# Expert weight slots fetched as two half transfers, each with its own semaphore and its own release

## The chip, the cores and the metric

One program on one core of a Trainium2 chip. The metric is the device time of one execution in microseconds; the times below are of three runs. The profile is of one further execution on the same kind of core, with the TensorE clock that was granted to it.

## What is computed

One decoder layer on 1024 tokens of width 1024, in float32. A first part mixes tokens (an RG-LRU branch, sliding-window attention, cross-attention to 256 memory tokens, one output projection). The second part, in which the change lies, is a mixture of 32 experts, four per token:

```python
def expert_block(args):                      # one block of up to 128 tokens of expert e
    xblk, e = args
    h = xblk @ w1[e] + b1[e]                 # w1[e]: 1024 x 2048
    return clamped_swiglu(h) @ w2[e] + b2[e] # w2[e]: 1024 x 1024

yb = lax.map(expert_block, (xb, block_expert)).reshape(P, D)
out = jnp.zeros((N, D), jnp.float32).at[tok_buf].add(yb.astype(jnp.float32) * gate_buf[:, None])
```

## The kernel before, in words

Each engine has an instruction stream written out by hand; semaphores tie them. From about 583 us a loop over passes runs on every engine (`Fori(0, total)`). A pass takes one expert and either one block of 128 tokens (`body((0,))`) or two (`body((0, 1))`), which is decided at run time by a table in SBUF. Here there are 32 passes, 19 with one block and 13 with two.

**Weights.** An expert is 12 MB: `NSLOT` = 12 slots of 1 MB, eight of w1 (four chunks of 128 rows by 512 columns) and four of w2 (two chunks of 128 rows by 1024 columns). A slot has two halves, `h = 2 * s` and `2 * s + 1`, and `part(h)` names the SBUF words of one. The raw words land in `ring`, which has room for `RAW` = 6 slots. SyncE (SP) issues a slot's transfer in `load_slot` (L379 to L385) and does nothing else in the loop: for each of the 12 slots it waits at L416 until the slot's place is free (`raw_done[s % RAW]`, counted up by one for each half), then issues (L385) with `slot_in[s % RAW]` as its semaphore. It works up to six slots ahead and goes on into the next pass's expert.

**Splitting.** A product in full precision is made of three float32r products. So each half is copied by ScalarE (ACT) into a rounded high part (`split_hi`, L760 to L769, into a ring of `SPLIT` = 8 buffers `w_hi`), after a wait for the slot's landing (L763) and for TensorE to have used the buffer (`w_used`, L765). VectorE (DVE) subtracts to get the low part (`split_lo`, L1688 to L1696, helper line L1643, into `w_lo`), and that operation counts `raw_done` up. Six halves at the start are split at L738 and L524. In passes with one block, slots 8 and 10 (`WHOLE`) aren't split: TensorE multiplies them as plain float32 straight out of `ring` (L1246), and releases the whole slot at its end by adding 2 to `raw_done` (L1248).

**TensorE (PE)** does per pass `up` or `up_turned` for w1, then `down` for w2. `wait_words` (L1158 to L1163) is its wait for a half: for `raw_done` or, where the slot is whole, for `slot_in`. The three products are L1138, L1139 and L1140.

**Tokens.** GpSimd (POOL) gathers the rows of the next pass, `xg`, by indirect DMA (L516) and adds the result rows to `out` by an indirect DMA that accumulates (the scatter, L549), in this order in a pass: `idx_cur` (L538), gather, scatter, wait for the scatter. TensorE transposes the gathered rows (L1132) after a wait at L1282 in the middle of the pass. The chain from the end of one pass is: ScalarE's `combine` writes `y` (L802), scatter, `idx_cur`, VectorE's `idx_next` (L1639), gather, transposes. All these transfers and the weights share the core's 16 DMA engines.

At the end VectorE waits for the transfers still in flight, one wait and one memset per semaphore (L1792 to L1794).

Of the kernel before, what the change touches and what calls it, by code (L numbers as in the profile page):

```python
# [40 lines left out]
HALF = 512  # L41
# [8 lines left out]
NSLOT = 12  # L50
NPART = 2 * NSLOT
RAW = 6
# [18 lines left out]
def hymba_layer(nc, x, mem, g_mix, w_in, conv_w, conv_b, lru_wa, lru_ba, lru_wx, lru_bx, lru_lambda,  # L71
# [3 lines left out]
    with ExitStack() as ctx:  # L75
# [3 lines left out]
        def sem(name):  # L79
            return ctx.enter_context(nc.semaphore(name))  # L80
# [25 lines left out]
        credit = sb("credit", [P, 16])  # L106
# [135 lines left out]
        ex_in, ex_done, mask_ready, pos_done, gates_ready, gt_done, gt_out, init_mm, init_ready = map(  # L242
            sem, "ex_in ex_done mask_ready pos_done gates_ready gt_done gt_out init_mm init_ready".split())
        ptab_ready, ttab_ps, ttab_ready = sem("ptab_ready"), sem("ttab_ps"), sem("ttab_ready")
        slot_in = [sem(f"slot_in{i}") for i in range(RAW)]
        hi_ready = sem("hi_ready")
        raw_done = [sem(f"raw_done{i}") for i in range(RAW)]
        w_used, y_half = sem("w_used"), sem("y_half")
# [74 lines left out]
        def slot(s):  # L323
            return ring[:, (s % RAW) * SLOT:(s % RAW + 1) * SLOT].rearrange("p (k c) -> p k c", k=4)
# [19 lines left out]
        @block.sync  # L344
        def _(sp):
            load_vectors(sp, 0)
            sp.dma_start(mem_sb, mem[0].rearrange("(t p) d -> p t d", p=P)).then_inc(mem_in, 16)
            xv = x[0].rearrange("(t p) d -> p t d", p=P)
            sp.dma_start(w_mem, w_mem_kv[0].rearrange("(k p) c -> p k c", p=P)).then_inc(w_mem_in, 16)
            sp.dma_start(xh[:, 0:4, :], xv[:, 0:4, :]).then_inc(x_in[0], 16)  # L350
            wv = w_in[0].rearrange("(k p) c -> p k c", p=P)
            def load_wA(i):
                sp.dma_start(wA[i], wv[:, :, i * DL:(i + 1) * DL]).then_inc(wA_in[i], 16)

            load_wA(0)
            sp.dma_start(xh[:, 4:8, :], xv[:, 4:8, :]).then_inc(x_in[1], 16)
            for i, (a, b, c) in enumerate(((384, 512, 1152), (0, 384, 768), (512, 768, 1408))):
                sp.dma_start(wB[:, :, a:b], wv[:, :, c:c + b - a]).then_inc(wB_in[i], 16)
            load_wA(1)

            sp.dma_start(wV, wv[:, :, 1280:1408]).then_inc(wout_in, 16)

            sp.wait_ge(normed, 2)
            sp.wait_ge(kz_zero, 5)
            for g in range(2):
                for half in range(2):
                    sp.dma_start(kz[g][half][half * DH:(half + 1) * DH, :],
                                 uT[g * DH:(g + 1) * DH, K, :]).then_inc(kz_in, 16)
            sp.wait_ge(spread, len(norm_units))
            sp.wait_ge(scanned, LT)  # L370
            for i in range(2):
                sp.dma_start(xh[:, 4 * i:4 * i + 4, :], xv[:, 4 * i:4 * i + 4, :]).then_inc(x_again[i], 16)
            sp.wait_ge(in_done, len(units))
            sp.dma_start(w_out_sb, w_out[0].rearrange("(k p) c -> p k c", p=P)).then_inc(wout_in, 16)

            w1v = w1[0].rearrange("e (k p) c -> e p k c", p=P)
            w2v = w2[0].rearrange("e (k p) c -> e p k c", p=P)

            def load_slot(e, s):  # L379
                if s < 8:  # L380
                    src = w1v[bass.ds(e, 1), :, 4 * (s % 2):4 * (s % 2) + 4, HALF * (s // 2):HALF * (s // 2) + HALF]
                else:
                    src = w2v[bass.ds(e, 1), :, 2 * (s - 8):2 * (s - 8) + 2, :]
                dst = slot(s) if s < 8 else slot(s).rearrange("p (k b) c -> p k (b c)", k=2)
                sp.dma_start(dst, src.rearrange("o p k c -> (o p) k c")).then_inc(slot_in[s % RAW], 16)  # L385


            sp.wait_ge(ylru, LT)
            sp.dma_start(gbc, g_ffn.to_broadcast([P, D])).then_inc(gbc_in, 16)

            sp.wait_ge(lru_ss, 1)
            sp.wait_ge(yt_out, ytc[-1])
            sp.wait_ge(o_ss, len(items))
            for s in range(4):
                load_slot(0, s)
            sp.wait_ge(op_done, 6 * NT)
            sp.wait_ge(padded, 2)
            sp.dma_start(b2_sb[0:E, :], b2[0]).then_inc(b2_in, 16)
            sp.wait_ge(b1_zero, 1)
            for half in range(2):  # L400
                sp.dma_start(b1_raw[half * E:(half + 1) * E, :], b1[0]).then_inc(b1_in, 16)
            sp.wait_ge(ttab_ready, 1)
            for s in range(4, RAW):
                load_slot(0, s)
            for i in range(NT):
                sp.wait_ge(init_ready, 2 * i + 2)
                sp.dma_start(out[0, i * P:(i + 1) * P, :], xh[:, i, :]).then_inc(init_out, 16)
            sp.wait_ge(init_out, 16 * NT)
            total = sp.value_load(ttab[0:1, TALL:TALL + 1], min_val=1, max_val=NPASS)
            with sp.Fori(0, total) as p:  # L410
                e_now = sp.value_load(ttab[0:1, bass.ds(p + TE, 1)], min_val=0, max_val=E - 1)
                e_next = sp.value_load(ttab[0:1, bass.ds(p + (TE + 1), 1)], min_val=0, max_val=E - 1)

                for s in range(RAW, RAW + NSLOT):

                    sp.wait_ge(raw_done[s % RAW], p * (NPART // RAW) + 2 * (s // RAW))  # L416
                    load_slot(e_now if s < NSLOT else e_next, s % NSLOT)

        @block.gpsimd
        def _(po):  # L420
# [143 lines left out]
        def _(act_e):  # L564
# [169 lines left out]
            act_e.wait_ge(w_used, SPLIT)  # L734
            act_e.preload_act_table(ACT.Gelu_apprx_sigmoid)
            for s in range(LEAD):
                act_e.wait_ge(slot_in[s // 2], 16)
                act_e.activation(halves_of(w_hi[s][:, :, :]), pairs_apart(part(s)), ACT.Copy).then_inc(hi_ready, 1)  # L738
            act_e.wait_ge(ttab_ready, 1)
            take_xhi(1, 0, 4)  # L740
# [9 lines left out]
            with act_e.Fori(0, total) as p:  # L750
# [6 lines left out]
                def body(groups):  # L757
                    whole = whole_of(groups)

                    def split_hi(s):  # L760
                        if s in whole:
                            return
                        act_e.wait_ge(slot_in[s % RAW], p32 + 16 * (s // RAW + 1))  # L763
                        for h in (2 * s, 2 * s + 1):
                            act_e.wait_ge(w_used, p24 + (h + 1 - (SPLIT if s - SPLIT // 2 in whole else 0)))  # L765
                            hi, raw = w_hi[h % SPLIT][:, :, :], part(h)
                            if s % NSLOT < 8:
                                hi, raw = halves_of(hi), pairs_apart(raw)
                            act_e.activation(hi, raw, ACT.Copy).then_inc(hi_ready, counted(h, whole))  # L769
# [62 lines left out]
        def _(pe):  # L832
# [313 lines left out]
            with pe.Fori(0, total) as p:  # L1146
# [8 lines left out]
                def body(groups):  # L1155
                    whole = whole_of(groups)

                    def wait_words(h):  # L1158
                        s = h // 2
                        if s in whole:  # L1160
                            pe.wait_ge(slot_in[s % RAW], p32 + 16 * (s // RAW + 1))
                        else:
                            pe.wait_ge(raw_done[s % RAW], uses + (2 * (s // RAW) + h % 2 + 1))  # L1163

# [143 lines left out]
        def _(dve):  # L1308
# [480 lines left out]
                with dve.Else():  # L1789
                    body((0,))  # L1790

            for i in range(RAW):  # L1792
                dve.wait_ge(slot_in[i], total * 32 + 16)
                dve.memset(credit[:, 8 + i:9 + i], 0.0)  # L1794


# [22 lines left out]
```

## Time and profile before

| | |
|---|---|
| three runs, us | 2244.38, 2245.2, 2251.28; median 2245.2 |
| profiled execution: its own time | 2243.14 us |
| profiled execution: span from first to last instruction | 2241.4 us |
| mean granted TensorE clock | 0.981 of full speed |
| TensorE busy | 2152.1 us (96% of the span) |
| VectorE, ScalarE busy | 1415.9 us, 1133.2 us |
| weight transfers issued by SyncE | 390 of 1024.0 KB, median 7.1 us from issue to landing |
| all DMA traffic | 477.64 MB, mean 213 GB/s |

The profile is of one execution. Busy times of engines overlap, so their sum says nothing; what matters is where TensorE, the busiest, stands idle and what ended the idle time. A matmul's end is modelled, so the spacing of starts tells its pace better than its duration. "Landing" is the time from a transfer's issue to its semaphore.

### The profile page before, as it was taken

The page shows a single profiled execution, that of the slowest core. Times are in us where ns is not written, and L with a number is a line of the kernel's source. Part 1 is how long each engine was busy: PE and PEld are TensorE (multiplying, and loading weights), DVE is VectorE, ACT ScalarE, POOL GpSimd, SP SyncE. Part 2 cuts the span into 40 slices and gives each one's busy share as a digit, 9 for nine tenths or more (in the row PEclk, how much of TensorE's full clock was granted, in tenths as well). Part 3 has the DMA queues.
Part 4 walks back from the last instruction along what each step waited for, and adds up shares of the span by engine and source line. Part 5 has one row for each costly group of instructions (what it writes and reads, how often), then busy time and mean ns, then how long its engine had stood idle before and what let it go on. Part 6 is the DMA issues. An engine that isn't in the chain of part 4 may idle for free.

```text
span 2241.4 us, 34981 instructions
## 1 busy us (share of the span) xinstructions
PE 2152.1 (96%) x11402; PEld 1675.3 (75%) x11403; DVE 1415.9 (63%) x2192; ACT 1133.2 (51%) x1570; POOL 217.6 (10%) x208
## 2 busy tenths in 40 slices
PE   6999988996999999999999999999999999999997
PEld 4443776443579977887797979887779888898895
DVE  3242574334676578768767676768886667667665
ACT  3241353112365567556646565556765555555555
POOL 2000200001300111010101010101110100101001
PEclk9999998996899999999999999999999999999998
DMA  7000402002696669968959595868998568659656
GB/s 260 1 0 19 160 1 76 28 29 71 241 349 236 215 218 359 335 207 319 370 210 312 190 322 181 316 195 310 353 351 299 192 204 295 200 181 319 190 191 218
DMA packets 203190, 477.64 MB, mean 213 GB/s; under 512 B 14743, under 2 KB 20951, under 8 KB 203088
## 3 DMA queue, kind: packets, MB, share of 16 engines
q1 hardware_dynamic: 185662, 437.95, 54.0%
q0 software_dynamic: 17424, 39.17, 7.3%
q8 instruction: 24, 0.39, 0.1%
q14 instruction: 14, 0.11, 0.0%
q10 hardware_dynamic: 66, 0.02, 0.0%
HBM read 468.73 MB, written 32.11 MB: 223 GB/s over the span
## 4 chain that ended last, share of the span: by engine, by line
PE 84%; DMA 7%; issue 3%; DVE 3%; ACT 2%; POOLq 1%; POOL 0%; ACTq 0%; DVEq 0%; SPq 0%
PE ps L1138 18%; PE ps L1140 18%; PE ps L1139 18%; PE ps L902 7%; PE ps L1246 6%; PE ps L1056 5%; DMA out<-y,idx_cur 3%; DMA xg<-token_rows,idx_next 3%; PE ps L1132 2%; PE ps L1007 1%; PE ps L975 1%; PE ps L1176 1%; PE ps L1196 1%; PE ps L1118 1%; PE ps L1075 1%
## 5 line engine op out<-in xcount | busy, mean ns | idle before, releaser
L769 ACT ACTIVATE w_hi<-ring 128x1024 fp32r<-128x1024 f32 x692 | 745.2, 1123 | 456.7 <-PE ps L1140 386.0
L1643 DVE TENSOR_TENSOR w_lo<-ring,w_hi 128x1024 fp32r<-128x1024 f32 x692 | 816.5, 1221 | 205.8 <-ACT w_hi L769 205.8
L1138 PE MATMUL ps<-xT,w_hi 128*128 128x256 f32 x1248 | 354.2, 284 | 0.0
L1140 PE MATMUL ps<-xT,w_lo 128*128 128x256 f32 x1248 | 353.1, 283 | 0.0
L1139 PE MATMUL ps<-xT,w_hi 128*128 128x256 f32 x1248 | 353.1, 283 | 0.0
L1138 PE MATMUL ps<-w_hi,xT 128*128 128x512 f32 x816 | 320.8, 393 | 6.3 <-issue 4.6
L1139 PE MATMUL ps<-w_lo,xT 128*128 128x512 f32 x816 | 319.8, 392 | 0.0
L1140 PE MATMUL ps<-w_hi,xT 128*128 128x512 f32 x816 | 319.3, 391 | 0.0
L1139 PEld LDWEIGHTS ps<-xT,w_hi 128*128 128x128 f32 x1248 | 239.5, 192 | 0.5
L1138 PEld LDWEIGHTS ps<-xT,w_hi 128*128 128x128 f32 x1248 | 239.4, 192 | 0.5
L1140 PEld LDWEIGHTS ps<-xT,w_lo 128*128 128x128 f32 x1248 | 239.4, 192 | 0.0
L1138 PE MATMUL ps<-w_hi,actT 128*128 128x512 f32 x568 | 231.9, 408 | 0.0
L1140 PE MATMUL ps<-w_hi,actT 128*128 128x512 f32 x568 | 221.9, 391 | 0.0
L1139 PE MATMUL ps<-w_lo,actT 128*128 128x512 f32 x568 | 221.4, 390 | 0.0
L549 POOL DMA_INDIRECT out<-y,idx_cur x45 | 82.8, 1840 | 1101.2 <-ACT y L802 1045.0
L1138 PEld LDWEIGHTS ps<-w_hi,xT 128*128 128x128 f32 x816 | 154.0, 189 | 41.7 <-DVE xT L1643 5.6
L1140 PEld LDWEIGHTS ps<-w_hi,xT 128*128 128x128 f32 x816 | 153.8, 188 | 32.9
L1139 PEld LDWEIGHTS ps<-w_lo,xT 128*128 128x128 f32 x816 | 153.7, 188 | 32.7
L1246 PE MATMUL ps<-ring,actT_f 128*128 128x512 f32 x304 | 136.7, 592 | 0.0
L1139 PEld LDWEIGHTS ps<-w_lo,actT 128*128 128x128 f32 x568 | 106.8, 188 | 25.6 <-issue 4.5
L1138 PEld LDWEIGHTS ps<-w_hi,actT 128*128 128x128 f32 x568 | 106.7, 188 | 25.2 <-issue 4.5
L1711 DVE TENSOR_SCALAR hm<-ps,km 128x256 f32<-128x256 f32 x156 | 64.7, 478 | 94.5 <-PE ps L1140 94.5
(274 smaller groups left out, 2417.4 us busy)
## 6 DMA issues: line engine op xcount, KB each, us to landing
ring<-in_w SPq DMA_DIRECT2D x390, 1024.0 KB, 7.1
xh<-in_x SPq DMA_DIRECT2D x4, 2048.0 KB, 15.5
work<-in_w_out SPq DMA_DIRECT2D x1, 4096.0 KB, 12.7
token_rows<-uT POOLq DMA_DIRECT2D x8, 512.0 KB, 2.9
out<-xh SPq DMA_DIRECT2D x8, 512.0 KB, 2.7
work<-in_w_in SPq DMA_DIRECT2D x2, 1536.0 KB, 18.4
uT<-in_w_mem_kv SPq DMA_DIRECT2D x1, 2048.0 KB, 13.8
ring<-in_w_in SPq DMA_DIRECT2D x1, 1536.0 KB, 18.4
```

The costliest lines, as they stand in the source:

```text
L549: po.indirect_dma_start(out=out[0], out_offset=by_index(idx_cur, g), in_=y[:, g, :], in_offset=None, bounds_check=last_row, oob_is_err=Fal ...
L769: act_e.activation(hi, raw, ACT.Copy).then_inc(hi_ready, counted(h, whole))
L902: m = pe.matmul(ps[:, unit_bank(i), :], w[:, k, :], xnT[:, k, h * HALF:(h + 1) * HALF], start=k == 0, stop=k == KD - 1)
L975: m = pe.matmul(ps[:, u % 4, n * 256 + lo:n * 256 + 256], qs, keys, start=True, stop=True)
L1056: m = pe.matmul(ps[:, 2 * g + half, :], uT[:, c, i * P:(i + 1) * P], w_out_sb[:, kk + n, half * HALF:(half + 1) * HALF], start=n == 0, sto ...
L1132: m = pe.transpose(ps[:, bank + k // 4, k % 4 * P:(k % 4 + 1) * P], xg[:, g, k * P:(k + 1) * P], ident[:, :])
L1138: pe.matmul(acc, hi, whi, start=first, stop=False, skip_group_check=shared)
L1139: pe.matmul(acc, hi, wlo, start=False, stop=False, skip_group_check=shared)
L1140: return pe.matmul(acc, lo, whi, start=False, stop=last, skip_group_check=shared)
L1246: m = pe.matmul(acc, actT_f[:, j + k, :], slot(s)[:, 2 * k + b, :], start=first, stop=last)
L1643: return dve.tensor_tensor(lo, x, hi.bitcast(F32), ALU.subtract)
L1711: m = dve.tensor_scalar(hm[:, g, j % 2, cols], ps[:, 2 * (j % 2) + g, cols], b1_cols[:, 4 * j + 2 * g + o, bass.ds(e, 1)], LIMIT + o, ALU. ...
```

## The change

A slot is now two transfers of 512 KB, one for each half. There are 12 semaphores `slot_in` in place of six, one for each half of the ring. SyncE waits for a half's release ahead of that half's transfer, ScalarE waits for a half's landing ahead of that half's copy, TensorE likewise for the unsplit slots. The bytes, their places in SBUF and all arithmetic are the same. The diff, with nothing but repeated context left out:

```diff
-        slot_in = [sem(f"slot_in{i}") for i in range(RAW)]
+        slot_in = [sem(f"slot_in{i}") for i in range(2 * RAW)]
...
-            def load_slot(e, s):
+            def load_half(e, h):
+                s = h // 2
                 if s < 8:
-                    src = w1v[bass.ds(e, 1), :, 4 * (s % 2):4 * (s % 2) + 4, HALF * (s // 2):HALF * (s // 2) + HALF]
+                    k0 = 4 * (s % 2) + 2 * (h % 2)
+                    src = w1v[bass.ds(e, 1), :, k0:k0 + 2, HALF * (s // 2):HALF * (s // 2) + HALF]
                 else:
-                    src = w2v[bass.ds(e, 1), :, 2 * (s - 8):2 * (s - 8) + 2, :]
-                dst = slot(s) if s < 8 else slot(s).rearrange("p (k b) c -> p k (b c)", k=2)
-                sp.dma_start(dst, src.rearrange("o p k c -> (o p) k c")).then_inc(slot_in[s % RAW], 16)
+                    src = w2v[bass.ds(e, 1), :, h - 16:h - 15, :]
+                return src.rearrange("o p k c -> (o p) k c")
+
+            def load_slot(e, s, freed=None):
+                for h in (2 * s, 2 * s + 1):
+                    if freed is not None:
+                        sp.wait_ge(raw_done[s % RAW], freed + h % 2)
+                    dst = part(h) if s < 8 else part(h).rearrange("p (k b) c -> p k (b c)", k=1)
+                    sp.dma_start(dst, load_half(e, h)).then_inc(slot_in[h % (2 * RAW)], 16)
...
-                    sp.wait_ge(raw_done[s % RAW], p * (NPART // RAW) + 2 * (s // RAW))
-                    load_slot(e_now if s < NSLOT else e_next, s % NSLOT)
+                    load_slot(e_now if s < NSLOT else e_next, s % NSLOT, p * (NPART // RAW) + (2 * (s // RAW) - 1))
...
             for s in range(LEAD):
-                act_e.wait_ge(slot_in[s // 2], 16)
+                act_e.wait_ge(slot_in[s], 16)
...
-                        act_e.wait_ge(slot_in[s % RAW], p32 + 16 * (s // RAW + 1))
                         for h in (2 * s, 2 * s + 1):
+                            act_e.wait_ge(slot_in[h % (2 * RAW)], p32 + 16 * (s // RAW + 1))
...
-                            pe.wait_ge(slot_in[s % RAW], p32 + 16 * (s // RAW + 1))
+                            pe.wait_ge(slot_in[h % (2 * RAW)], p32 + 16 * (s // RAW + 1))
...
-            for i in range(RAW):
+            for i in range(2 * RAW):
                 dve.wait_ge(slot_in[i], total * 32 + 16)
-                dve.memset(credit[:, 8 + i:9 + i], 0.0)
+                if i % 2:
+                    dve.memset(credit[:, 8 + i // 2:9 + i // 2], 0.0)
```

How the streams stand, first SyncE in its loop, at slots 6, 7 and 8 (`raw_done0` to `raw_done2` are the places of the ring, 128x4x512 is partitions x chunks x columns; L385 is the line of the issue). Before:

```order
L385 ISA [waits raw_done0]
L385 DMA ring<-in_w 128x4x512
L385 ISA [waits raw_done1]
L385 DMA ring<-in_w 128x4x512
L385 ISA [waits raw_done2]
L385 DMA ring<-in_w 128x2x1024
```

The same three slots with the change, where the issue has line L393:

```order
L393 ISA [waits raw_done0]
L393 DMA ring<-in_w 128x2x512
L391 REGISTER_ALU
L393 ISA [waits raw_done0]
L393 DMA ring<-in_w 128x2x512
L393 ISA [waits raw_done1]
L393 DMA ring<-in_w 128x2x512
L393 ISA [waits raw_done1]
L393 DMA ring<-in_w 128x2x512
L393 ISA [waits raw_done2]
L393 DMA ring<-in_w 128x1024
L393 ISA [waits raw_done2]
```

Each transfer has become two with a wait ahead of each, and the rows that one moves are as long as before (512 or 1024 words). Then ScalarE in its loop, at the splits of slots 4 and 5 in a pass with two blocks. Before, one wait for a slot and a register operation without a wait ahead of its second half:

```order
L769 ACTIVATE w_hi<-ring 128x1024 [waits w_used]
L765 REGISTER_ALU [waits slot_in5]
L769 ACTIVATE w_hi<-ring 128x1024 [waits w_used]
L765 REGISTER_ALU
L769 ACTIVATE w_hi<-ring 128x1024 [waits w_used]
```

With the change (L772 and L776 are the same two statements):

```order
L776 ACTIVATE w_hi<-ring 128x1024 [waits w_used]
L772 REGISTER_ALU [waits slot_in10]
L776 ACTIVATE w_hi<-ring 128x1024 [waits w_used]
L772 REGISTER_ALU [waits slot_in11]
L776 ACTIVATE w_hi<-ring 128x1024 [waits w_used]
```

The second register operation now holds the wait for the second half; no instruction has been added or moved in the loop. TensorE's, VectorE's and GpSimd's compute instructions stand in the same order as before.

## Rows read from the trace of the kernel before

**Rows 1.** The page, part 1: busy time, share of the span, instructions.
```profile
PE 2152.1 (96%) x11402; PEld 1675.3 (75%) x11403; DVE 1415.9 (63%) x2192; ACT 1133.2 (51%) x1570; POOL 217.6 (10%) x208
```

**Rows 2.** Expert loop: length, busy (x) of PE, PEld, DVE, ACT, POOL; clock, DMA share, GB/s.
```profile
600.00:2227.00 1627.00, 1621.06 (x9312) 1360.15 (x9310) 1152.81 (x1688) 949.91 (x1176) 154.05 (x139) 1.00 0.76 264
```

**Rows 3.** TensorE's waits from 600 us on: us in total, times, longest.
```profile
PE ps L1132 <- DMA xg<-token_rows,idx_next: 4.1, 7, 1.3
PE ps L1138 <- DVE hm L1716: 1.2, 1, 1.2
```

**Rows 4.** The chain that ended last: start, us, what (first, steady run, last).
```profile
612.66 3.44 PE ps L1246 x8
...
1599.46 3.44 PE ps L1246 x8
...
1636.88 3.43 PE ps L1246 x8
...
1665.09 8.82 DMA xg<-token_rows,idx_next
1675.04 3.44 PE ps L1246 x8
...
2214.28 3.44 PE ps L1246 x8
```

**Rows 5.** ScalarE's waits for weights over the whole span.
```profile
ACT w_hi L769 <- DMA ring<-in_w: 57.3, 32, 4.6
```

**Rows 6.** Steady single-block passes, columns as in rows 2.
```profile
1551.00:1588.50 37.50, 37.50 (x174) 28.21 (x173) 30.74 (x44) 26.14 (x32) 3.85 (x4) 1.00 0.97 357
...
1626.00:1663.50 37.50, 37.50 (x174) 28.17 (x173) 30.84 (x44) 26.19 (x32) 3.93 (x4) 1.00 0.94 347
```

**Rows 7.** DMA view from 1575 to 1595 us; GB/s in 40 slices of 0.5 us.
```profile
GB/s 414 418 410 397 401 393 385 393 393 389 389 369 381 320 312 340 357 360 369 410 397 414 438 397 451 401 401 410 410 410 434 401 434 401 393 401 410 406 398 406
DMA packets 3100, 7.91 MB, mean 395 GB/s; under 512 B 240, under 2 KB 240, under 8 KB 3100
...
q1 hardware_dynamic: 2871, 7.49, 96.4%
...
ring<-in_w SPq DMA_DIRECT2D x8, 1024.0 KB, 12.2
xg<-token_rows,idx_next POOLq DMA_INDIRECT x2, 7.6
```

**Rows 8.** SyncE's waits from 600 us on.
```profile
SPq L385 <- DVE w_lo L1643: 1078.3, 248, 9.6
SPq L385 <- PE ps L1246: 283.7, 38, 12.4
```

**Rows 9.** Tile ring, then line L385: ns min/median/max, first and last start; landing in us.
```profile
L1643 DVE TENSOR_TENSOR w_lo<-ring,w_hi x692: 1205/1220/1286, 589.8 to 2226.8; 128x1024 fp32r<-128x1024 f32 x173
...
L385 SPq DMA_DIRECT2D ring<-in_w x390: 368/373/829, 376.7 to 2225.1; - x195
...
DMA to landing us min/median/max: 4.7/7.1/15.1
```

**Rows 10.** SyncE in order of time, 1612.4 to 1614.2 us.
```profile
1612.51 1.78 SPq L385 DMA_DIRECT2D ring<-in_w  x3
```

**Rows 11.** Landing of the gather (tile xg), then of the scatter (tile out), from 600 us.
```profile
DMA to landing us min/median/max: 3.1/5.9/8.9
...
DMA to landing us min/median/max: 6.0/7.9/9.6
```

**Rows 12.** TensorE's weight loads ahead of the transposes, from the waits.
```profile
PEld ps L1132 <- DMA xg<-token_rows,idx_next: 8.3, 10, 1.8
```

**Rows 13.** The end: VectorE and GpSimd in order of time.
```profile
2232.39 0.06 DVE L1794 MEMSET credit<- 128x1 f32 x1 [2.61 <-DMA ring<-in_w]
...
2228.67 1.62 POOL L549 DMA_INDIRECT out<-y,idx_cur  x1 [23.08 <-ACT y L802]
```

**Rows 14.** The page, part 6: a 512 KB transfer, KB, median us to landing.
```profile
out<-xh SPq DMA_DIRECT2D x8, 512.0 KB, 2.7
```

## The prediction

> **What bounds the kernel now.** I read the page's totals first, then busy time by stretch, then the waits, and at the end single passes.
>
> The page [rows 1] gives TensorE 2152.1 of 2241.4 us. By stretch [rows 2], the expert loop from 600 to 2227 us holds 1621.06 busy of 1627.00, at a granted clock of 1.00. So TensorE stands idle there for 1627.00 - 1621.06 = 5.9 us, and its waits [rows 3] name nearly all of it: 4.1 us in seven waits for the gathered token rows xg and 1.2 us in one for hm. No wait for a weight is in that list. A busy figure can hide a slow cadence, so I also looked at the chain of waits in a run of passes with one block each [rows 4]: the first eight fp32 matmuls of L1246 of a pass start at 1599.46 and 1636.88, a period of 37.4 us. The next ones start at 1675.04, 38.2 us later; this pass was held up, and by the gather that stands before it in the chain, which landed at 1665.09 + 8.82 = 1673.91.
>
> Who does wait for weights? ScalarE, 57.3 us in 32 waits, the longest 4.6 us [rows 5]. It may be 8 halves ahead of TensorE (the rings w_hi and w_lo), and none of these waits comes out on TensorE. The DMA engines are closer to a limit than the page's mean says: 0.76 busy over the loop [rows 2], but 0.97 to 0.94 in the three steady passes of the run [rows 6], of which the first and the last stand there. In a stretch of 20 us the rate stays between 312 and 451 GB/s with some seven slots passing through [rows 7]. SyncE mostly waits for a free slot: 1078.3 + 283.7 = 1362 of the loop's 1641 us [rows 8].
>
> So there are two quantities near a limit: TensorE, and in runs of single-block passes the DMA engines, on which also hangs the chain y, scatter, gather, transposes.
>
> **The change part by part.**
>
> *Twice the transfers.* 390 become 780, 24 in a pass in place of 12. The order of instructions shows the same bytes in the same row lengths (128x2x512 for 128x4x512, 128x1024 for 128x2x1024), so the engines' data packets are as many. On SyncE an issue takes 0.373 us [rows 9], and three in a row with their register work 1.78 us [rows 10], 0.6 us each. 12 more in each of 32 passes make 384 x 0.6 = 230 us, against 1362 us of waiting: SyncE's queue hides it. A half moves for about 512 KB / 395 GB/s = 1.3 us (the rate from [rows 7]), twice its issue, so a burst stays limited by the engines, too. Were this cover gone, 12 x 0.6 = 7 us a pass would show.
>
> *What a boundary between transfers costs on the engines.* No row shows it alone. From below: zero, for in [rows 7] whole half-microsecond slices stand at 401 to 451 GB/s and no dip recurs every 2.6 us. From above: charge all that the 20 us lack against the fast slices of some 415 GB/s, (415 - 395) / 415 = 5%, or 1.0 us, to 7.5 boundaries: 0.13 us each. Twelve more in a pass are then 0 to 1.6 us of engine time. The steady passes have 3 to 6% of 37.5 us free, 1.1 to 2.2 us. I take zero, as the slices without a dip are the nearest row; even the upper end just fills what is free.
>
> The Trainium skill ("DMA: Bandwidth & Descriptors", section Rules for kernel authors) speaks against the change: it asks for at least 1 MiB per DMA, and its Anatomy section puts a fixed 2.0 us on each. Its formula would give 4.4 us for a slot and 2 x 3.2 = 6.4 us for two halves, an estimate from that page, if they went one by one; the trace does not agree that this sets the pace, since twelve slots pass in 37.5 us with other traffic beside them.
>
> *The release by half.* VectorE's two w_lo operations on a slot take 1.22 us each [rows 9], and SyncE no longer waits for the second: the first half of a slot is asked for about 1.2 us sooner. Not so for slots 8 and 10 of single-block passes, which the matmuls of L1246 release as a whole (38 of SyncE's waits, [rows 8]). The data starts sooner only where engines are idle at that time.
>
> *The wait by half.* ScalarE can split a first half when that has landed, some 1.3 us before its slot would have. That can take up to 32 x 1.3 = 42 us out of its 57.3 us. By the order of instructions it costs nothing: the register operation ahead of the second half now carries the wait that it lacked, and no row is added. What does it give TensorE? Nothing directly, since TensorE never waits for a weight. Indirectly, VectorE's low parts come sooner behind ScalarE's high ones, again ahead of need. The one wait for hm is the only place where this could reach TensorE.
>
> *What could shift on the path.* Scatter and gather. The gather's landing ranges from 3.1 to 8.9 us, median 5.9; the scatter's from 6.0 to 9.6, median 7.9 [rows 11]. Weight traffic that starts 1.2 us sooner also ends sooner where a refill runs out during the gather. At best all 4.1 + 1.2 = 5.3 us go. At worst every critical gather is like the slow ones: in the steady run it landed in 7.6 us [rows 7], in the pass that was held up in 8.8 [rows 4]; 1.2 us more at each of the 10 single-block passes in which the transposes' weight loads already wait for it [rows 12], 12 us. I take -0.5 us: the traffic at those places is saturated in both kernels, and bytes per pass are the same.
>
> *Prologue and end.* The first slot is issued at 376.7 us [rows 9], long ahead of the loop; nothing waits for the first halves. At the end the last two refills are issued by 2225.1, VectorE takes the second at 2232.39 [rows 13], and the kernel closes with a scatter issued at 2228.67, which at the shortest landing of a scatter, 6.0 us [rows 11], is still under way at 2235. Two issues more are 2 x 0.6 = 1.2 us, in front of something that has over 2 us to spare. Zero; if the cover were gone, 1.2 us.
>
> **Sum.** 0 (issue) + 0 (boundaries) + 0 (ScalarE's waits) - 0.5 (gather) + 0 (end) = -0.5 us. The profiled execution took 2243.14 us by its own time, so it would take 2242.6. The median of the three runs is 2.1 us above that execution; against it the forecast is 2244.7 us. 0.3% of the time is 6.7 us, as much as the three runs spread (2244.38 to 2251.28), and about what a measurement tells from no change. So: no change.
>
> **Rivals.**
>
> 1. *The gather pays (slower).* Halves asked for sooner keep weight packets queued at the very time the scatter and the gather want the 16 engines. Place: the wait for xg at L1282 in single-block passes. Price: up to 1.2 us in 10 passes, 12 us, 2257 us. It decides from the point where scatter and gather together land over 0.7 us later, for 10 x 0.7 is 7 us. For it: in the steady run the transposes come right as the gather lands. Against it: weight traffic is at 96% there already [rows 7], and cannot crowd more.
>
> 2. *The boundary costs (slower).* If a boundary took 0.25 us, twelve would be 3.0 us against about 1.6 free: 1.4 us for each of the 9 single-block passes that follow another such pass, 13 us, 2257 us (19 such passes start between 612.66 and 2214.28, [rows 4], in ten runs, the longest of five). It needs twice my upper bound. Driven to its end, with each transfer waiting for the one before, it would be 24 x 2.7 us (the landing of a 512 KB transfer, [rows 14]) = 65 us for a single-block pass in place of 37.5, some 19 x 27 = 520 us, 2765 us. But by that reading the kernel before would need 12 x 4.7 (the shortest landing of a slot, [rows 9]) = 56 us for a pass, and it takes 37.5; I give this end 0.005. It is what the Trainium skill's fixed cost per DMA, named above, would mean here.
>
> 3. *Relief (faster).* The sooner loads end before the gather does and clear its waits wholly, 5.3 us, with a shorter last scatter perhaps 7 us: 2238 us. For it: the waits are there. Against it: the share of the engines stays 0.94 and more.
>
> 4. *The change does not do what it says.* A half is free early only where VectorE frees it; if VectorE's pair comes back to back and the queue of weights is deep anyway (12.2 us to land in the steady run, [rows 7]), the sooner request buys nothing. The time is then 2245.2, within the forecast.
>
> **Chances.** Forecast with rival 4: 0.78. Gather pays 0.09, boundary costs 0.05 (its end of 2765 us, 0.005, within), relief 0.08. Range: from relief, 2238, to the slower rivals, 2257. Faster by over 0.3% 0.08, within 0.3% 0.78, slower 0.14.
>
> **What would show it.** Right: TensorE idle between 600 and 2227 us still 5 to 7 us, no wait for a weight; 772 or more weight issues at 0.37 us; period of single-block passes 37.4 us; ScalarE's waits for ring down from 57 towards 20 to 40 us; landing of a transfer in the steady run barely shorter, as it is made of queue. Wrong: the landing of gather or scatter up by over 0.5 us at the median and more than 10 us of waits at L1132 (rival 1), or a rate in the steady run below 380 GB/s and waits of TensorE for w_lo or ring (rival 2), or those waits gone (rival 3).

## The result, and the profile after

The change makes the kernel slower: 2265.1 us (median of 7 runs, 2256.33 to 2270.78) against 2245.2 us (7 runs, 2244.05 to 2253.48). The ratio on record is 1.0072, 95% interval 1.0052 to 1.0091, which is 16 us of 2245; the two medians stand somewhat further apart, 19.9 us. The forecast was no change, 2244.7 us, and its range ended at 2257.

The page of the changed kernel, against [rows 1]:

```profile
span 2267.1 us, 36209 instructions
...
PE 2164.6 (95%) x11402; PEld 1683.3 (74%) x11403; DVE 1415.0 (62%) x2192; ACT 1135.7 (50%) x1570; POOL 220.8 (10%) x208
```

The span of this one execution is 25.7 us longer than before. It is one of the slower of the seven (2268.82 us by its own time), and not all of the difference belongs to the change. The chain of waits shows where the loop begins and ends, by the first and the last group of L1253 (L1246 before):

```profile
620.74 3.44 PE ps L1253 x8
...
2246.29 3.45 PE ps L1253 x8
```

Before, the first was at 612.66 [rows 4] and the last group of all at 2220.91, so the loop took 1608.3 us; now it takes 2246.29 - 620.74 = 1625.6 us, 17.3 us more. That agrees with the measured 0.72% (16 us). The other 8.1 us came ahead of the loop, where the compute instructions are unchanged. What differs there is the granted TensorE clock: in the first 600 us it is 0.94 in the profile before and 0.92 here. Over all fourteen profiles of this document the start of the first group goes with it: 610.5 to 615.3 us in the six profiles with 0.94, 617.1 to 619.2 us in the six with 0.93, 618.1 and 620.7 us in the two with 0.92. So the loop is what to compare.

TensorE's waits in the loop, as in [rows 3]:

```profile
PE ps L1145 <- DVE hm L1723: 10.4, 7, 3.9
PE ps L1139 <- DMA xg<-token_rows,idx_next: 7.5, 7, 1.6
```

The wait for `hm` has gone from 1.2 us in one place to 10.4 us in seven, that for the gathered rows from 4.1 to 7.5. Together that is 12.6 us of the 17.3. There is still no wait for a weight.

Part of the rest is again the granted clock. The longest wait for `hm`, 3.9 us, is this one:

```profile
1869.13 0.80 PE L1145 MATMUL ps<-w_hi,xT 128*128 128x512 f32 x1 [3.87 <-DVE hm L1723]
```

From 1868.2 us on, while TensorE still waits, the granted clock is 0.50, the lower of the two levels (1.2 in place of 2.4 GHz), for 6.8 us. The same columns as in [rows 2]:

```profile
1868.30:1875.00 6.70, 5.87 (x15) 4.66 (x16) 6.70 (x16) 3.00 (x5) 1.02 (x1) 0.50 0.94 298
```

Before, the loop has no such stretch. At half the clock 6.8 us can cost up to 3.4 us, an estimate, which leaves 1.3 us unplaced. It isn't a loss of every execution: the repeat below has no such stretch in its loop, which is 16.0 us longer than before. Some 3.4 us of that lie outside the listed waits, and no view places them.

Who holds up `hm`? VectorE, in order, stood at `pad` (L1637, now L1644), the first step of `idx_next`, until GpSimd had copied `idx_cur`, which it does when the scatters have landed. Before, then after:

```profile
DVE pad L1637 <- POOL idx_cur L538: 37.8, 18, 4.4
```

```profile
DVE pad L1644 <- POOL idx_cur L545: 59.6, 18, 7.2
```

The landing of the gather, then of the scatter, against [rows 11] (3.1/5.9/8.9 and 6.0/7.9/9.6):

```profile
DMA to landing us min/median/max: 4.7/7.0/8.8
...
DMA to landing us min/median/max: 6.1/9.4/11.6
```

Both take longer: the gather 1.1 us at the median, the scatter 1.5 us.

**One place.** This is the two-block pass that the one wait for `hm` of before followed. It is the extreme case: of the 13 two-block passes it takes the longest from the last scatter to `idx_cur`, before (10.85 us) and after (13.57). GpSimd and VectorE in order of time, before:

```profile
1832.04 1.62 POOL L549 DMA_INDIRECT out<-y,idx_cur  x1 [52.23 <-issue]
1833.96 1.58 POOL L549 DMA_INDIRECT out<-y,idx_cur  x1 [0.30 <-issue]
1844.81 0.19 POOL L538 TENSOR_TENSOR idx_cur<-idx_next,no_index 128x2 int32<-128x2 int32 x1 [9.27 <-issue]
...
1845.13 0.16 DVE L1637 TENSOR_SCALAR pad<-ps 128x2 f32<-128x2 f32 x1 [4.37 <-POOL idx_cur L538]
...
1847.70 0.69 DVE L1716 TENSOR_TENSOR hm<-ps,limit 128x512 f32<-128x512 f32 x1
```

The same place after:

```profile
1850.00 1.62 POOL L556 DMA_INDIRECT out<-y,idx_cur  x1 [52.23 <-issue]
1851.93 2.63 POOL L556 DMA_INDIRECT out<-y,idx_cur  x1 [0.31 <-issue]
1865.50 0.19 POOL L545 TENSOR_TENSOR idx_cur<-idx_next,no_index 128x2 int32<-128x2 int32 x1 [10.94 <-issue]
...
1865.82 0.16 DVE L1644 TENSOR_SCALAR pad<-ps 128x2 f32<-128x2 f32 x1 [7.17 <-POOL idx_cur L545]
...
1868.39 0.68 DVE L1723 TENSOR_TENSOR hm<-ps,limit 128x512 f32<-128x512 f32 x1
```

From the first scatter to `idx_cur` it was 12.8 us and is 15.5; VectorE's wait grew from 4.37 to 7.17, and `hm` comes 18.4 us after the first scatter in place of 15.7. Of these 2.7 us, up to 1.05 us can be the second scatter's issue on GpSimd itself (2.63 us in place of 1.58). The other 12 two-block passes have no such difference: there the second issue takes 2.3 to 2.5 us in both kernels. The rest is told by SyncE. Before, it issued slot 9 at 1835.41, 3.4 us after the first scatter's issue; now slot 9's first half goes at 1852.13, 2.1 us after it. When the scatters are issued, nothing moves here: the rate in 40 slices of 0.5 us, before (from 1830 us) and after (from 1848 us):

```profile
GB/s 442 410 385 0 0 0 0 0 131 82 156 180 213 197 189 131 164 197 311 336 336 279 360 352 401 418 360 344 360 401 434 418 361 303 229 188 182 92 177 389
```

```profile
GB/s 320 131 0 0 0 0 0 0 131 74 123 188 205 238 164 279 352 270 262 287 295 352 295 320 303 344 344 361 344 385 434 385 352 279 246 221 123 25 0 0
```

The DMA view of three microseconds that begin 5 us after the first scatter's issue, about when the first weight packets move, before (1837 to 1840 us) and after (1855 to 1858 us); q0 is GpSimd's queue, q1 SyncE's, the last number the share of the 16 engines:

```profile
q0 software_dynamic: 124, 0.24, 57.6%
q1 hardware_dynamic: 104, 0.43, 41.8%
```

```profile
q1 hardware_dynamic: 200, 0.76, 71.9%
q0 software_dynamic: 27, 0.05, 8.3%
```

Before, the second scatter and the weights started together and shared the engines. After, the weights were running when the second scatter became ready, and for some 3 us GpSimd's queue moved next to nothing. (The view doesn't tell the two scatters' packets apart; that the few of q0 are the end of the first is read from their times.) The same 3 us show elsewhere. By the start times of q0's packets in the trace before, the first one follows the issue of a scatter by 5.0 to 5.2 us in the 18 one-block passes that another pass follows, where five weight transfers are under way, and by 2.2 us after the first scatter of all 13 two-block passes, where one or none is. (In the last pass two are under way, and it is 2.7 us.) And the shift of slot 9 is the same in every two-block pass but this: its issue comes 2.2 to 2.4 us after the second scatter's before and 1.1 to 1.2 us after it now (1.45 and 0.20 us here).

That is theory A: the early half takes the engines in the gap between the two scatters of a two-block pass.

The Trainium skill ("DMA: Bandwidth & Descriptors", section Queues, rings and completion order) says that each engine goes round the queues that have work, a packet at a time. The trace agrees once both queues run, as before from 1837 us on. In the first microseconds of a transfer that comes behind a running one there is no such sharing (8.3% against 71.9%); whether the scatter's queue already had packets to offer then, no view shows.

**The rest of what was to be seen.** ScalarE still waits as long for weights, in twice as many pieces (57.3 us in 32 before):

```profile
ACT w_hi L776 <- DMA ring<-in_w: 58.7, 66, 4.3
```

SyncE's waits:

```profile
SPq L393 <- DVE w_lo L1650: 900.3, 450, 8.5
SPq L393 <- PE ps L1253: 254.2, 38, 12.4
```

SyncE waits 1154.5 us in place of 1362. Its time outside waits, from 600 us to the end, went from 279 to 513 us: the added issues took some 233 us, and its waiting still covers them.

### The profile page after: what moved, and what is told of

The parts are those of the page before. It is cut to its first block, busy times and chain, and to the rows that moved or that the text cites. A ratio compares the mean times of both kernels' runs of the same rounds, so it can differ in the third digit from the quotient of the medians.

```text
span 2267.1 us, 36209 instructions
## 1 busy us (share of the span) xinstructions
PE 2164.6 (95%) x11402; PEld 1683.3 (74%) x11403; DVE 1415.0 (62%) x2192; ACT 1135.7 (50%) x1570; POOL 220.8 (10%) x208
## 4 chain that ended last, share of the span: by engine, by line
PE 81%; DMA 8%; issue 3%; DVE 3%; ACT 2%; POOLq 1%; POOL 0%; DVEq 0%; ACTq 0%; SPq 0%
PE ps L1145 17%; PE ps L1146 17%; PE ps L1147 17%; PE ps L909 7%; PE ps L1253 6%; PE ps L1063 5%; DMA out<-y,idx_cur 5%; DMA xg<-token_rows,idx_next 3%; PE ps L1139 2%; PE ps L1014 1%; PE ps L982 1%; PE ps L1183 1%; PE ps L1203 1%; PE ps L1082 1%; PE ps L1125 1%
## 5 line engine op out<-in xcount | busy, mean ns | idle before, releaser
L776 ACT ACTIVATE w_hi<-ring 128x1024 fp32r<-128x1024 f32 x692 | 748.4, 1124 | 448.2 <-PE ps L1147 376.3
L1145 PE MATMUL ps<-w_hi,xT 128*128 128x512 f32 x816 | 322.6, 395 | 15.8 <-DVE hm L1723 10.4
L1253 PE MATMUL ps<-ring,actT_f 128*128 128x512 f32 x304 | 136.7, 592 | 0.0
L784 ACT ACTIVATE gel<-hm 128x256 f32<-128x256 f32 x180 | 73.2, 413 | 112.1 <-DVE hm L1723 97.7
## 6 DMA issues: line engine op xcount, KB each, us to landing
xh<-in_x SPq DMA_DIRECT2D x4, 2048.0 KB, 15.5
work<-in_w_out SPq DMA_DIRECT2D x1, 4096.0 KB, 12.8
work<-in_w_in SPq DMA_DIRECT2D x2, 1536.0 KB, 17.9
```

The costliest lines, as they stand in the source:

```text
L784: act_e.activation(gel[:, g, j % 2, :], hm[:, g, j % 2, 0:HALF // 2], ACT.Gelu_apprx_sigmoid).then_inc(gel_ready[g], 1)
L1145: pe.matmul(acc, hi, whi, start=first, stop=False, skip_group_check=shared)
L1253: m = pe.matmul(acc, actT_f[:, j + k, :], slot(s)[:, 2 * k + b, :], start=first, stop=last)
```

## The experiments

Each ratio below is against the kernel before, timed beside it, with its 95% interval. One statistic is used throughout beside the waits: the time from the start of a pass's last scatter (L549) to the start of `idx_cur` (L538), worked out from their starts in the trace and averaged over the 18 one-block and the 13 two-block passes that another pass follows. It is 10.9 us and 9.6 us before, 11.5 and 11.6 us with the change. Where a loop's length is given, it is from the first to the last group as above, of one profile each; the repeats of a kernel differ by 1.3 us or less.

**The changed kernel again** (no edit).

> The changed kernel once more, beside the three edits of it. Theory A (the release by half sends weights off about 1.2 us sooner, so that they are running before GpSimd's second scatter of a two-block pass is ready; its first packet then comes some 3 us later) and theory B (twice as many transfers slow the software queue, whenever they are issued) both expect 1.005 to 1.009 of before, the scatter's median landing at 9.4 us against 7.9, and the chain to the first L1253 matmul of the last pass about 17 us longer.

Ratio 1.0076 (1.0056 to 1.0095); scatter's median landing 9.5 us; hm 9.3 us, xg 8.6 us; scatter to `idx_cur` 11.5 us in one-block passes and 11.6 in two-block ones. As expected, it repeats; the loop is 16.0 us longer than before, where 17 were expected.

**Halves, with the release of the whole slot.**

```diff
-                        sp.wait_ge(raw_done[s % RAW], freed + h % 2)
+                        sp.wait_ge(raw_done[s % RAW], freed + 1)
```

> Half transfers, but both of a slot wait for the release of the whole slot, as before. Theory A: weights leave as late as before, the scatter's median landing falls back to 7.9 to 8.2 us, TensorE's waits for hm and xg to about 5 us, the time to within 0.2% of before. Theory B: the count of transfers is unchanged from the changed kernel, so the scatter stays at 9.4 us and the time at 1.005 to 1.009.

Ratio 1.0029 (1.0014 to 1.0045). Its waits:

```profile
PE ps L1139 <- DMA xg<-token_rows,idx_next: 9.2, 9, 1.7
PE ps L1145 <- DVE hm L1723: 3.1, 1, 3.1
```

The scatter's median is 8.3 us, and two-block passes are back to 10.2 us. But one-block passes stay at 11.5 us, the two waits come to 12.3 us where theory A expected about 5 (17.9 with the change), and 0.3% remains where it expected at most 0.2. The loop is 7.7 us longer than before. So theory A carries the larger part, and theory B some: neither alone.

**Release by half, landing of the whole slot.** ScalarE waits for both halves ahead of the first copy.

```diff
                         for h in (2 * s, 2 * s + 1):
                             act_e.wait_ge(slot_in[h % (2 * RAW)], p32 + 16 * (s // RAW + 1))
+                        for h in (2 * s, 2 * s + 1):
```

> Release by half kept, but ScalarE waits for both halves of a slot before it copies the first. Theory A: ScalarE's copies come later, which delays releases a little only where it waits for weights; scatter still near 9.4 us, time 1.005 to 1.009. A theory C, that ScalarE's earlier or more numerous waits cause the loss, expects the time back at that of before.

Ratio 1.0085 (1.0066 to 1.0103), the scatter at 9.4 us. ScalarE's waits for weights grew to 72.9 us in 32 places, and the time didn't fall: theory C is out, and so is any use of the earlier landing beyond the interval.

**The gate.** The changed kernel, in which SyncE issues slot 9 only after GpSimd has issued the scatters of the pass before (a memset behind them counts up a semaphore that is otherwise done with; its count stands at 6 as the loop begins).

```diff
                 for s in range(RAW, RAW + NSLOT):
-
+                    if s == 9:
+                        sp.wait_ge(zeroed, p + 6)
...
                                               compute_op=ALU.add).then_inc(scattered[g], 16)
 
+                    po.memset(sentt[:, :], 0.0).then_inc(zeroed, 1)
```

> The changed kernel, with one more wait of SyncE: slot 9's first half of each pass is issued only once GpSimd has issued the scatters of the pass before. Theory A: in two-block passes the second scatter is then ready before the weights run; its first packet comes some 3 us sooner, idx_cur starts 9.5 to 10 us after the second scatter in place of 11.6, the waits for hm go (10.4 to under 2 us), time 0.998 to 1.003 of before. Theory B: no change from the changed kernel, 1.005 to 1.009, or slower by the delayed weights.

Ratio 1.0017 (1.0003 to 1.0031). Its waits:

```profile
PE ps L1143 <- DMA xg<-token_rows,idx_next: 7.0, 8, 1.5
```

```profile
DVE pad L1648 <- POOL idx_cur L548: 36.7, 18, 3.1
```

The waits for `hm` are gone altogether, the time from scatter to `idx_cur` in two-block passes falls to 9.0 us, VectorE's wait is back at what it was, and the loop is 1.7 us longer than before. One-block passes stay at 11.5 us. This run sends weights off later than the changed kernel and wins 0.6%, which no theory of late weights can give.

**Only one of the matrices in halves.** `load_slot` takes the whole-slot form for the others, with one semaphore for the slot; waits follow.

```diff
+        def split_slot(s):
+            return s % NSLOT < 8          # the w1 run; s % NSLOT >= 8 in the w2 run
...
+                if not split_slot(s):
+                    if freed is not None:
+                        sp.wait_ge(raw_done[s % RAW], freed + 1)
...
+                    sp.dma_start(dst, src.rearrange("o p k c -> (o p) k c")).then_inc(slot_in[2 * (s % RAW)], 16)
+                    return
```

> Only the eight slots of w1 go in halves (with release and landing by half); the four of w2 go whole, as before. Theory A (early start of slot 9 ahead of the second scatter) expects most of the loss gone, for slot 9 is w2: from the last scatter of a two-block pass to idx_cur 9.6 to 10.3 us in place of 11.6, waits for hm 0 to 3 us, time 1.001 to 1.004 of before. A theory D, that each halved slot costs the same, expects two thirds of the loss: 1.005.

> Only the four slots of w2 go in halves, the eight of w1 whole. Theory A: idx_cur still 11 to 11.7 us behind the second scatter, hm waits of 6 to 10 us, time 1.004 to 1.007. Theory D: one third of the loss, 1.0025.

With w1 in halves: 1.0037 (1.0019 to 1.0055), two-block passes 9.7 us, one-block passes 11.5 us. With w2 in halves: 1.0035 (1.0022 to 1.0047), 11.5 us and 11.0 us. First the w1 run's waits, then the w2 run's:

```profile
PE ps L1166 <- DMA xg<-token_rows,idx_next: 14.1, 11, 2.2
PE ps L1172 <- DVE hm L1751: 0.7, 1, 0.7
```

```profile
PE ps L1172 <- DVE hm L1751: 9.0, 8, 2.1
PE ps L1166 <- DMA xg<-token_rows,idx_next: 4.9, 8, 1.6
```

The waits come apart: halves of w2 hurt the second scatter of two-block passes (hm), halves of w1 the scatter and gather of one-block passes (xg). The times decide less: both came out at half of the loss. For w1, 1.0037 lies in theory A's range (1.001 to 1.004); for w2, 1.0035 lies under its 1.004 to 1.007. Theory D's 1.005 and 1.0025 both lie within the intervals, so these two ratios don't exclude it; what speaks against it is that the two kinds of pass react to different slots, and the next two runs. The loops are 12.0 and 10.6 us longer than before, and with w1 in halves the waits come to 14.8 us, more than the 12.3 with full release everywhere. So the early release of w1 slots may cost something of its own, which no run here isolates.

**Slot 9 alone, both ways.** In the first, of all slots only slot 9 has the full release; in the second, only slot 9 has the early one.

```diff
-                        sp.wait_ge(raw_done[s % RAW], freed + h % 2)
+                        sp.wait_ge(raw_done[s % RAW], freed + (1 if s == 9 else h % 2))   # first run
+                        sp.wait_ge(raw_done[s % RAW], freed + (h % 2 if s == 9 else 1))   # second run
```

> The changed kernel, but slot 9's first half, and no other, waits for the release of its whole slot. Theory A says that this one transfer's early start is what hits the second scatter: idx_cur 9.6 to 10.3 us behind the second scatter of two-block passes in place of 11.6, waits for hm at most 3 us, and the time half way back, 1.002 to 1.005, like the run with full release everywhere (1.0029). If the early start of all slots matters, nothing changes: 11.6 us and 1.0075.

> The mirror image: halves with full release everywhere, but slot 9's first half goes off early. Theory A: idx_cur back at 11.3 to 11.7 us, waits for hm 7 to 10 us, time 1.005 to 1.008. Otherwise as with full release everywhere: 10.2 us and 1.003.

Slot 9 late: 1.0033 (1.0019 to 1.0047), two-block passes 10.3 us. Slot 9 alone early: 1.0061 (1.0040 to 1.0081), 11.5 us. VectorE's wait, first run and second:

```profile
DVE pad L1644 <- POOL idx_cur L545: 48.4, 18, 6.5
```

```profile
DVE pad L1644 <- POOL idx_cur L545: 59.4, 18, 5.3
```

TensorE waits 3.2 us for `hm` in the first and 9.2 us in the second. The loops are 12.4 us longer than before (of which up to 3.4 us are again a stretch of 6.8 us at a granted clock of 0.50, behind the 3.2 us wait) and 15.3 us longer. One transfer of 24, sent 1.2 us sooner in each pass, makes the difference between full release (1.0029) and early release (1.0072 and 1.0076) as far as the intervals tell. The number of halves is the same in all these runs, so theory D, by which each halved slot costs the same, is out.

**The number of transfers alone.** The kernel before, with a second transfer of 128 bytes behind each slot.

```diff
+                if used is not None:
+                    sp.wait_ge(tiny_in[s % RAW], used)
+                sp.dma_start(tiny[0:16, 2 * (s % RAW):2 * (s % RAW) + 2], w_router[0, 0:16, 0:2]).then_inc(tiny_in[s % RAW], 16)
```

> The kernel before with whole transfers, and behind each a second one of 128 bytes (16 partitions of two words of w_router) with a semaphore of its own: as many transfers as the changed kernel, but no half. It asks for the source of what the full-release run left (loop 1618.9 us against 1611.3, idx_cur 0.6 us later in one-block passes). If the number of transfers and their semaphore writes does it, idx_cur comes 11.3 to 11.5 us after the scatter in one-block passes and the time is 1.002 to 1.004; if it is the data moved in half-size pieces, 10.9 us and 0.999 to 1.001.

Ratio 1.0025 (1.0009 to 1.0041); one-block passes 11.4 us, two-block ones 9.8 us. Its waits:

```profile
PE ps L1137 <- DMA xg<-token_rows,idx_next: 6.5, 7, 1.6
PE ps L1143 <- DVE hm L1721: 3.4, 1, 3.4
```

Whole slots, no early release, and yet the scatter of one-block passes is as late as with halves; the loop is 5.9 us longer than before. No wait of SyncE for a small transfer shows in its trace. So the part that full release leaves (1.0029) is best explained by the added transfers as such, though the intervals of the two runs are wide. How a transfer of 128 bytes delays a scatter wasn't tested further.

**A version that beats both.** The gate in the kernel before, with whole slots, at slot 9, run twice, and at slot 7.

> The kernel before, whole transfers, with the gate: slot 9 of a pass is issued only once GpSimd has issued the scatters of the pass before. Theory A: there slot 9 went off only just behind the second scatter's issue already, so little is left to win: idx_cur 9.0 to 9.6 us behind the second scatter, the one wait for hm of 1.2 us gone, time 0.998 to 1.001 of before.

> The kernel before with the gate at slot 9 once more, on another visit to the chip, since its gain of 0.2% is small. If it is real: 0.997 to 0.999 of before, interval below 1, idx_cur 8.7 to 9.1 us behind the second scatter of two-block passes. If it was the spread between loads of a program: 0.999 to 1.001.

> The kernel before with the gate two slots earlier, at slot 7: in one-block passes, too, some weights then wait until the scatter has been issued. If a scatter that finds the weight queue empty is worth more than the weights' delay, idx_cur comes 9 to 10.5 us after the scatter in one-block passes too (10.9 before) and the time is 0.996 to 0.998; if the two or three slots queued ahead of it already decide, one-block passes stay at 10.9 us, and later weights in the runs of one-block passes, where the engines are 0.94 to 0.97 busy, can cost: 0.997 to 1.003.

At slot 9: 0.9980 (0.9969 to 0.9991) and again 0.9980 (0.9966 to 0.9994); the loops are 2.8 and 2.1 us shorter than before. The first expectation asked for little (9.0 to 9.6 us, 0.998 to 1.001) and the runs gave a little more: two-block passes 8.8 and 8.9 us, and these waits in the first of the two runs:

```profile
PE ps L1136 <- DMA xg<-token_rows,idx_next: 3.8, 5, 1.3
```

```profile
DVE pad L1641 <- POOL idx_cur L541: 30.0, 18, 2.9
```

At slot 7: 0.9999 (0.9986 to 1.0011). One-block passes stay at 10.8 us, and the first packet of a scatter still follows its issue there by 5.0 us, which fits the expectation that the slots already queued decide. The weights come late: ScalarE waits 131.9 us for them, TensorE's waits for the gathered rows rise to 8.6 us. Of the two places tried, the gate pays just ahead of the transfer that collides and not two slots sooner.

## Why the prediction was wrong

**What bounds the kernel**: right. TensorE does, its idle time was about six microseconds, mostly waits for hm and xg, no weight is ever late for it, and the chain y, scatter, gather, transposes stands right behind. Of the 17.3 us lost in the profiled loop, 12.6 are waits on this chain and up to 3.4 are the granted clock behind one of them.

**Twice the transfers**: the cost on SyncE was sized at 230 us and measured some 233; it showed nowhere on TensorE. The boundary on the engines was put at zero, by looking at the rate alone. The rate did hold over whole passes: 361, 347 and 347 GB/s in three steady ones against 357 and 347 [rows 6]. A stretch of 20 us of the steady run has these slices (1592 to 1612 us, against [rows 7]); its mean is 376 GB/s against 395, under the 380 that the prediction had named as a sign of rival 2, but the lack is in the first two slices:

```profile
GB/s 139 279 344 393 328 340 356 369 377 393 381 360 344 320 361 308 332 336 352 365 393 422 410 426 426 410 434 410 418 410 418 410 426 401 401 426 393 420 406 391
```

But added transfers cost something else, the landing of GpSimd's transfers beside them, worth 0.25 to 0.3% (tiny transfers, full release; the intervals go from 0.09 to 0.45%). This term, set to 0, measures some 6 us. The rule of at least 1 MiB per DMA in the Trainium skill ("DMA: Bandwidth & Descriptors", section Rules for kernel authors) pointed the right way. The fixed cost of each transfer, which the prediction took from the page's Anatomy section, isn't how it came about here: the period of a steady pass is unchanged (1579.43 to 1616.87 us, 37.4 us). The prediction also applied it further than the page does, which gives that fit for transfers issued from GpSimd, while the weights are issued from SyncE.

**The release by half** was right in what it does (1.2 us sooner) and wrong in where: "The data starts sooner only where engines are idle at that time" is exactly the place of the loss, and I didn't go and look which place that is.

**The wait by half**: wrong in size, harmless. 20 to 40 us of ScalarE's waits were to be left, and 58.7 us are, in 66 waits in place of 32. The second half now is waited for, too; that this makes up for what the first half gains is our reading of the count.

**What could shift on the path** is the step that failed: "I take -0.5 us: the traffic at those places is saturated in both kernels". That was read from one-block passes alone. In a two-block pass the engines are idle or nearly so when the scatters are issued, SyncE's next transfer is the only one about, and 1.2 us decide whether it comes with or ahead of the second scatter. In place of -0.5 us the term measures +7 to 11 us (1.0072 to 1.0076 less 1.0029, times 2245, is 9.7 to 10.6 us; slot 9 alone gives 1.0076 less 1.0033, 9.7 us, and 1.0061 less 1.0029, 7 us). It was priced by the wait for xg only; it is paid through VectorE, which stands in order at `pad` behind the scatter while `hm` waits behind it. I had written of that wait for hm that it was "the only place where this could reach TensorE", and had then looked only at what it could gain.

**Rivals.** Rival 1 had the right kind of mechanism, scatter and gather landing later because weights go off sooner, and a price of 12 us where some 16 were lost. It had the wrong place (one-block passes, xg: 3.4 us) and got a chance of 0.09 by the argument that saturated engines can't crowd more. That its price is near the loss is luck, for it was added up over other passes. Of its two signs one came: gather and scatter land 1.1 and 1.5 us later at the median, but the waits for xg are 7.5 us and not over 10. Rival 2 had the sign of the smaller part and not its way: over whole passes no rate fell, and no wait for w_lo or ring appeared. Rivals 3 and 4 are out.

**Prologue and end**: right as far as can be seen. From the last group of L1253 to the end it is 20.8 us, 20.5 before, and the start of the loop goes with the granted clock.

## What to carry to other kernels

A transfer that is asked for sooner isn't free where a transfer of another queue that the bounding engine does depend on is about to start: before you call a prefetch harmless, look, for each kind of pass, at what the engines do in the microseconds in which it will now begin, and which in-order engine stands behind what it delays. Where weights have slack and a scatter or gather has none, try letting the weights wait until the small transfer has been issued; here one such wait per pass makes the kernel 0.2% faster, and moved two slots ahead it gives that back. Splitting transfers bought nothing here, where TensorE never waits for them. And compare the stretch that the change touches: ahead of the loop the profiles differ by up to 10 us (610.5 to 620.7 us at the first group), and that goes with the granted clock, not with the change.

## What the runs showed of the hardware that was not expected

- A scatter that finds weights running moves nearly nothing for about 3 us (8.3% of the engines against 71.9%; first packet 5.0 us after the issue in 18 one-block passes against 2.2 us in 13 two-block passes), where one that starts with them shares from the start (57.6% against 41.8%). Why wasn't tested.
- Behind the longest wait of TensorE, 3.9 us, the granted clock was 0.50 for 6.8 us. Waits of 3.2 us in the run with slot 9 late and 3.4 us with the tiny transfers also have such a stretch behind them (6.8 and 3.4 us), the one of 3.1 us with full release has none.
- 12 transfers more in a pass make the time from scatter to `idx_cur` in one-block passes 0.5 us longer though they carry only 128 bytes each (10.9 to 11.4 us).
- The issue of a second scatter on GpSimd takes 2.3 to 2.5 us in 12 of the 13 two-block passes, in both kernels, where a first scatter's takes 1.6. The exception is the place shown above, before the change, with 1.58; it takes 2.63 there with the change, and also with full release. What makes an issue long is open.
